# A hybrid decoder step on one core: semaphore clears and one memset moved into the programs of running stages, first weights and first norm started earlier

## The chip, the cores and the metric

The kernel runs on one core of a Trainium2 chip. Its time is the device time of one execution in microseconds (us); the median of several runs is compared. An engine's program is a list of instructions that it takes in order; engines wait for each other by semaphores. PE is TensorE, DVE VectorE, ACT ScalarE, POOL GpSimd, and SP SyncE, which here only issues transfers (DMAs).

## What is computed

One inference step of a one-layer decoder, for a prompt group (1024 tokens) and a sample group (8 sequences of 4 tokens with a paged cache of 4096 keys) that share all weights. All of it is in float32:

```
xn = rmsnorm(x);  [A | B] = groups of xn @ w_in
h  = x + concat(DSA_A(xn), DiffAttn_B(xn)) @ w_out
h2 = h + MemXAttn(rmsnorm(h), mem)
y  = h2 + ConvFFN(rmsnorm(h2))
rmsnorm(x, g) = x * rsqrt(mean(x*x) + 1e-6) * g
```

DSA_A is attention over the 256 keys that an indexer scores highest, DiffAttn_B the difference of two softmax attentions with relative-position bias. Rows of projected keys and values are outputs too.

## The kernel before

The work is a row of stages. Each stage is one block: every engine gets its own program for it, and at the block's end all engines meet (each drains, POOL collects them and releases them) before any starts the next block. The stages up to the feed-forward part are "in" (the input projection), "pb" (prompt differential attention), "sa" (prompt selective attention beside all sample attention), "wo" (output projection, residual, norms of its result and of the memory tokens), "kv" and "mq" (memory projections), then the attention into the memory and its projection.

Semaphores of a stage are made by `Stage.sem`, which appends them to the list `Stage.ended`. Twice, after pb and after sa, `clear_semaphores` (line 177) opens a block of its own in which POOL alone has work, one clear instruction for each semaphore of the list. After wo a third small block holds one DVE memset of QBM, a [128, 1024] tile that the mq stage fills in part (line 3364).

The input projection (`projection_stage` with `first_norm`) goes through steps (chunk of columns j, tile of 128 tokens t), 9 tiles for each chunk; the first chunk is 324 columns wide. A step is 8 pairs of fp32 matmul instructions on PE (the trace counts 16). Interleaved with steps are two helpers:

- `FirstNorm` makes the normalised, transposed input XT tile by tile. ACT squares and sums a tile of x, POOL makes 1/sqrt of the mean, DVE scales the tile (`scale`, line 480) into one of two buffers in KTB, PE transposes it in two halves (line 496) into two PSUM banks, DVE copies each half out and multiplies by the norm's gains (line 468). Tiles 0 to 4 are turned before step 0, tile s + 4 ahead of step s.
- `Setup` loads constants, turns 124 rows of per-column gains into columns (`turn_columns`, `columns`) and makes tables: bias rows for 12 heads, one head per step, on PE (line 332) and DVE (line 363), and page tables for the gathers. It waits for its loads with the semaphore `loaded`.

SP issues in this order: 13 small loads counted by `first` (identity, norm and gain rows), 13 loads counted by `loaded` (two pieces of a constant table, relative bias, gains, lambda, the page table), then the first chunk of w_in in four pieces, piece x when tile x is scaled, because these weights lie where x tiles 0 to 3 lie. ACT issues the nine x tiles, on a queue of its own.

The order of all this is fixed by the Python loops: what stands in a step of a helper comes at that step, on each engine.

Of the kernel before, what the change touches and what calls it, by code (L numbers as in the profile page):

```python
# [22 lines left out]
P = 128  # L23
D = 1024
# [152 lines left out]
def clear_semaphores(nc):  # L177

    with nc.Block() as block:
        @block.gpsimd  # L180
        def _(pool):
            for s in Stage.ended:
                pool.sem_clear(s)
    Stage.ended.clear()

# [27 lines left out]
class Setup:  # L213
# [7 lines left out]
    def __init__(self, nc, ctx, io, M, K):  # L221
# [6 lines left out]
        def place(n):  # L228
# [13 lines left out]
        self.first, self.loaded = S.sem("first"), S.sem("loaded")  # L242
        self.toe_out = [S.sem(f"toe_out{x}") for x in range(4)]
        (self.chain, self.cols_tr, self.rbw_ready, self.bias_mm, self.bias_cp, self.lrow_ready, self.samp_mm,
         self.lam_ready, self.lam_exp) = (S.sem(n) for n in (
             "chain", "cols_tr", "rbw_ready", "bias_mm", "bias_cp", "lrow_ready", "samp_mm", "lam_ready", "lam_exp"))
        self.n_first = self.n_loaded = 0

    def first_loads(self, sp):
# [5 lines left out]

        def rowload(name, src, k):
            load(self.rows[COL[name]:COL[name] + k, :], src.rearrange("(k p) -> k p", p=P))
        load(M.ident[:], io["ident"][:])
        rowload("norm_mix", io["norm_mix"][0], KC)
# [29 lines left out]
    def turn_columns(self, pe):  # L289
        pe.wait_ge(self.first, self.n_first)  # L290
        self.nc.tensor.transpose(self.M.PS[:, 4, 0:NCOL], self.rows[:], self.K("ident")[0:NCOL, 0:NCOL]
                                 ).then_inc(self.cols_tr, 1)

    def columns(self, dve):
# [8 lines left out]
        link(nc.vector.tensor_copy(M.cols[:], M.PS[:, 4, 0:NCOL]))  # L303
# [50 lines left out]
    def dve(self, eng, s, room):  # L354
        nc, M, K = self.nc, self.M, self.K
        link, h = self.link, s - 1
# [3 lines left out]
        if 0 <= h < self.HEADS:  # L360
# [4 lines left out]
        if s == 0:  # L365
# [47 lines left out]
class FirstNorm:  # L413
# [3 lines left out]
    AHEAD = 4  # L417

    def __init__(self, nc, ctx, io, M, K, setup):
# [8 lines left out]
    def sp(self, eng):  # L428
        self.setup.first_loads(eng)
        self.setup.other_loads(eng)  # L430

    def act(self, eng):
        nc, M = self.nc, self.M
        load_x(eng, self.io, M)
        junk = M.PS[:, 0:2, :].rearrange("p b n -> p (b n)")
        for t in range(NT):
# [4 lines left out]
            nc.scalar.activation(junk[0:n, :], M.X[0:n, t, :], ACT.Square,  # L441
# [14 lines left out]
    def dve(self, eng, s):  # L456
# [5 lines left out]
        for t in range(self.copied, min(NT, s + self.AHEAD + 1)):  # L462
# [3 lines left out]
            for b in range(2):  # L466
# [3 lines left out]
                    M.PS[:, 6 + b, 0:4 * n].rearrange("p (c n) -> p c n", c=4),  # L470
# [12 lines left out]
    def pe(self, eng, s):  # L483

        nc, M = self.nc, self.M
        if s == 0:
            self.setup.turn_columns(eng)
        for t in range(self.turned, min(NT, s + self.AHEAD + 1)):
            n = rows_of(t)
            eng.wait_ge(self.scaled, t + 1)  # L490
            for b in range(2):
                if t:
                    eng.wait_ge(self.evac_done, 2 * t - 1 + b)
                for c in range(4):
                    k = 4 * b + c
                    last = nc.tensor.transpose(M.PS[:, 6 + b, c * n:(c + 1) * n],
# [3 lines left out]
        if s == 0:  # L500
            eng.wait_ge(self.sq_done, NT)
# [4 lines left out]
def projection_stage(nc, M, K, name, XT, kc, tiles, w_dram, chunks, w=None, sq=None, beside=None, ahead=None,  # L506
                     following=None, first_norm=None):
# [20 lines left out]
    with ExitStack() as ctx:  # L528
# [20 lines left out]

        def wait_nat(eng, s):  # L550
# [7 lines left out]
        with nc.Block() as block:  # L558
            @block.sync
            def _(sp):  # L560
                def load(j):
# [5 lines left out]
                    if j == 0:  # L567
                        for x, first in enumerate(w_first):
                            if first_norm:
                                sp.wait_ge(first_norm.scaled, x + 1)  # L570
                            sp.dma_start(w[0][:, 2 * x:2 * x + 2, 0:c.width],
# [8 lines left out]
                if first_norm:  # L580
                    first_norm.sp(sp)
                load(0)
# [19 lines left out]
            def _(pe):  # L602
# [15 lines left out]
                for s, (j, t) in enumerate(steps):  # L618
# [9 lines left out]
                    for c in range(kc):  # L628
                        if s == 0 and c == 0 and ahead:
                            pe.wait_ge(*ahead[1:])  # L630
                        elif s == 0 and c % 2 == 0 and not ahead:
                            pe.wait_ge(w_first[c // 2], 16)
                        last = nc.tensor.matmul(M.PS[0:n, s % 3, 0:chunks[j].width],  # L633
                                                XT[:, c, t * P:t * P + n], w[j % 2][:, c, 0:chunks[j].width],
# [881 lines left out]
def selective_and_sample_stage(nc, io, M, K):  # L1516


    with ExitStack() as ctx:
# [1903 lines left out]
```

## Time and profile before

| | us |
|---|---|
| median of 3 runs | 2669.65 (2663.4 to 2672.65) |
| profiled execution, its time | 2665.05 |
| its span | 2663.2 |
| PE busy | 2344.6 (88%) |
| DVE busy | 1105.1 (41%) |
| ACT busy | 767.4 (29%) |
| POOL busy | 725.6 (27%) |

The span is the time from the first to the last instruction of the profiled execution, 1.85 us less than its time. The granted clock of PE was 0.94 of full over the span. A line number with q behind the engine's name (PEq, SPq) is that engine's sequencer: branches, waits and issues of transfers. "Landing" is when a transfer's semaphore has been raised.

### The profile page before, as it was taken

The numbers are of one execution on the slowest core, as the hardware profiler recorded it, in microseconds if no ns is written. First come the engines' busy times: TensorE is split into PE (matmuls) and PEld (weight loads), VectorE is DVE, ScalarE is ACT, GpSimd is POOL, SyncE is SP. The second block draws the span as 40 slices with busy tenths as digits, with TensorE's granted clock in tenths as the row PEclk, the third lists the DMA queues.
The fourth block names the chain that finished last, engine by engine and source line by source line (L and its number), as shares of the span: only waits on it lengthen the run. The fifth ranks groups of instructions, "written<-read, shape, count | busy, mean of one in ns | idle before, by whom it ended". The sixth has DMA issues, their size and how long they took to land. (4 is left out here: it accounts for less than half of the span.)

```text
span 2663.2 us, 32560 instructions
## 1 busy us (share of the span) xinstructions
PE 2344.6 (88%) x12153; PEld 1563.1 (59%) x12173; DVE 1105.1 (41%) x2683; ACT 767.4 (29%) x2065; POOL 725.6 (27%) x767
## 2 busy tenths in 40 slices
PE   7999997767887887877669989898999999999999
PEld 5644444443554555544444434547888888888887
DVE  4489988732445533232321311335334334352001
ACT  3551346643444444433331102411111111110000
POOL 1450222123445454436430001003212212201110
PEclk9999997988889898888789999999999999999999
DMA  3211101035888687755433022220111111122221
GB/s 136 73 60 68 35 7 64 1 111 185 273 270 280 215 276 259 249 159 162 124 111 144 0 79 79 80 81 33 49 40 42 49 33 49 49 63 68 72 62 41
DMA packets 148611, 281.75 MB, mean 106 GB/s; under 512 B 14487, under 2 KB 83783, under 8 KB 148455
## 3 DMA queue, kind: packets, MB, share of 16 engines
q0 software_dynamic: 49408, 176.19, 20.3%
q1 hardware_dynamic: 80758, 90.50, 10.3%
q10 hardware_dynamic: 18288, 12.98, 1.7%
q8 instruction: 99, 1.62, 0.3%
q14 instruction: 58, 0.47, 0.1%
HBM read 261.68 MB, written 17.94 MB: 105 GB/s over the span
## 5 line engine op out<-in xcount | busy, mean ns | idle before, releaser
L633 PE MATMUL PS<-region 128*128 128x512 f32 (+5 forms) x864 | 327.7, 534 | 1.4 <-DMA region<-w_in 1.4
L2730 PE MATMUL PS<-region,ffn_w 128*128 128x264 f32 x1408 | 323.3, 388 | 1.6 <-PEq L2181 1.6
L2730 PEld LDWEIGHTS PS<-region,ffn_w 128*128 128x128 f32 x1408 | 269.3, 191 | 48.6 <-issue 2.0
L1962 ACT COPY region<-PS 128x512 f32<-128x512 f32 x352 | 197.9, 590 | 231.2 <-remote 74.3
L633 PEld LDWEIGHTS PS<-region 128*128 128x128 f32 (+1 forms) x864 | 152.7, 181 | 160.8 <-issue 140.5
L1841 PE MATMUL PS<-ident_f,region 128*128 128x128 f32 x1024 | 173.0, 318 | 81.5 <-ACT region L1962 45.7
L2730 PE MATMUL PS<-region,side 128*128 128x264 f32 x1056 | 243.3, 387 | 1.6 <-POOL side L2687 1.6
L2730 PEld LDWEIGHTS PS<-region,side 128*128 128x128 f32 x1056 | 198.9, 190 | 35.0 <-POOL side L2687 1.7
L1841 PEld LDWEIGHTS PS<-ident_f,region 128*128 128x128 f32 x1024 | 134.6, 163 | 117.0 <-issue 75.4
L930 DVE TENSOR_SCALAR_CACHE_REDUCE mask<-score,cand 128x384 bf16<-128x384 f32 (+2 forms) x198 | 180.9, 942 | 3.4
L1108 POOL DMA_INDIRECT region<-cache_b_k,gather_b x128 | 121.8, 952 | 217.3 <-PE PS L1841 180.2
L2685 POOL TENSOR_TENSOR side<-ffn_w 128x512 f32<-128x512 f32 x22 | 28.8, 1307 | 391.4 <-DMA ffn_w<-w_gate 197.6
L2877 DVE TENSOR_TENSOR ffn_gb<-PS,ffn_u 128x264 f32<-128x264 f32 (+2 forms) x66 | 20.5, 338 | 181.5 <-ACT ffn_u L2841 118.7
L2250 PE MATMUL PS<-side,QTB 128*128 128x512 f32 x192 | 87.1, 604 | 0.9 <-PEq L2606 0.9
L1108 POOL DMA_INDIRECT region<-cache_a_v,gather_a x64 | 61.7, 964 | 95.1 <-PE PS L1924 70.8
L2097 DVE SCALAR_TENSOR_TENSOR sa_oacc<-sa_oacc,sa_alpha,PS 128x512 f32<-128x512 f32 (+1 forms) x48 | 29.5, 614 | 135.4 <-PE PS L1924 101.7
L2320 DVE TENSOR_TENSOR region<-PS,region 128x512 f32<-128x512 f32 (+1 forms) x36 | 24.8, 689 | 137.7 <-PE PS L2250 137.7
L1477 DVE TENSOR_REDUCE sa_a_far_max<-PS 128x1 f32<-128x16 f32 (+6 forms) x56 | 31.9, 569 | 103.2 <-PE PS L1418 81.0
L1108 POOL DMA_INDIRECT region<-cache_b_v,gather_b x64 | 60.3, 941 | 42.8 <-PE PS L1924 20.6
L3066 PE MATMUL PS<-H,ffn_w 128*128 128x264 f32 x308 | 69.8, 386 | 1.3 <-PEq L2674 1.3
L2810 ACT COPY side<-PS 128x264 f32<-128x264 f32 x44 | 16.7, 379 | 181.7 <-PE PS L2730 181.7
L1238 ACT ACTIVATE region<-PS,pb_negmax 128x384 f32<-128x384 f32 (+5 forms) x96 | 54.6, 578 | 49.3 <-DVE pb_negmax L1332 32.3
(444 smaller groups left out, 4023.8 us busy)
## 6 DMA issues: line engine op xcount, KB each, us to landing
ffn_w<-w_gate SPq DMA_DIRECT2D x11, 1024.0 KB, 5.4
ffn_w<-w_up SPq DMA_DIRECT2D x11, 1024.0 KB, 5.5
region<-w_in SPq DMA_DIRECT2D x4, 2048.0 KB, 7.9
ffn_w<-w_down ACTq DMA_DIRECT2D x7, 704.0 KB, 5.6
region<-x_prompt ACTq DMA_DIRECT2D x8, 512.0 KB, 7.1
region<-x_prompt SPq DMA_DIRECT2D x8, 512.0 KB, 11.4
mem_keys<-cache_mem_k SPq DMA_DIRECT2D x8, 512.0 KB, 4.2
mem_values<-cache_mem_v SPq DMA_DIRECT2D x8, 512.0 KB, 7.6
```

Source lines behind the costliest of these rows:

```text
L633: last = nc.tensor.matmul(M.PS[0:n, s % 3, 0:chunks[j].width], XT[:, c, t * P:t * P + n], w[j % 2][:, c, 0:chunks[j].width], start=(c == 0 ...
L930: self.link.send(nc.vector.tensor_scalar(self.mask[:, sc], self.score[:, sc], as_float[:, x:x + 1], 0.0, op, ALU.add, accum_out=self.count ...
L1108: nc.gpsimd.indirect_dma_start(out, None, src, bass.IndirectOffsetOnAxis(ap=table[:, col:col + 1], axis=0)).then_inc(arrived, 16)
L1238: nc.scalar.activation(prob[:, 2 * (n % 2) + k, a:b], slot(piece0[n] + x, b - a)[:, k], ACT.Exp, bias=negmax[:, n % 2, k:k + 1], accum_out ...
L1477: nc.vector.tensor_reduce(far_max[:, e:e + 1], slot(e, 0, lo), axis=AX.X, op=ALU.max).then_inc(far_done, 1)
L1841: last = nc.tensor.transpose(t[:, q * P:(q + 1) * P], keys[:, r * 512 + m * P:r * 512 + (m + 1) * P], K("ident"))
L1962: nc.scalar.copy(dst, M.PS[0:dst.shape[0], T0 + x % 2, 0:dst.shape[1]]).then_inc(t_read, 1)
L2097: nc.vector.scalar_tensor_tensor(oacc[:, 0:kw], oacc[:, 0:kw], alpha[:, x], M.PS[:, L1, 0:kw], ALU.mult, ALU.add).then_inc(o_done, 1)
L2250: last = nc.tensor.matmul(M.PS[:, s % 4, :], lhs(c, t), w[q][:, c, :], start=(c == 0), stop=(c == kc - 1))
L2685: nc.gpsimd.tensor_tensor(ws[:, 0], a21, a22, ALU.add).then_inc(made, 1)
L2730: last = nc.tensor.matmul(M.PS[:, bank, 0:TW], left[:, c, :], right[:, c, :], start=begin and c == 0, stop=(c == KH - 1), skip_group_check ...
L3066: last = nc.tensor.matmul(M.PS[:, bank + x, 0:TW], left[:, c, :], right[:, c, x * TW:(x + 1) * TW], start=begin and c == 0, stop=(c == KH ...
```

## The change

- `clear_semaphores` and both of its blocks are gone. The semaphores that had ended before sa are cleared at the end of POOL's program in sa (58, where there were 56: two semaphores are new); those of sa at the start of POOL's program in wo (38).
- The memset of QBM moves from its own block on DVE to the start of POOL's program in wo.
- The first chunk's weights go to the place of QTA (turned queries, written later in the same stage) and not over x. They need not wait for tiles, and SP issues them third, before the loads of `loaded`.
- The norm_mix rows (8) are turned by themselves, after two loads only; the other 116 columns are turned at step 2, after 11 loads counted by a new semaphore `rest`, which SP issues last.
- Two tiles are turned before step 0 and two more ahead of each step up to step 3, with four PSUM banks for the first three tiles; ACT's squares write their unused result to QTB and not to PSUM.
- The part of `Setup` that DVE did at step 0 is at step 1, together with what was there; bias rows of heads 0 and 1 are both made there.

```diff
@@ Setup
+        load(M.ident[:], io["ident"][:])
+        load(self.rows[0:KC, :], io["norm_mix"][0].rearrange("(k p) -> k p", p=P))
+    def rest_loads(self, sp):
...
+    def turn_columns(self, pe, k):
+        pe.wait_ge(*((self.first, self.n_first) if k == KC else (self.rest, self.n_rest)))
@@ Setup.pe
+        if s == 2:
+            self.turn_columns(eng, NCOL)
@@ Setup.dve
-        if s == 0:
+        if s == 1:
             eng.wait_ge(self.loaded, self.n_loaded)
...
+        if s == 2:
+            self.other_columns(eng)
+        for h in (0, 1) if s == 1 else range(s, min(s + 1, self.HEADS)) if s else ():
@@ FirstNorm
-        junk = M.PS[:, 0:2, :].rearrange("p b n -> p (b n)")
+        self.junk = M.QTB[:].rearrange("p m n -> p (m n)")[:, 0:D]
+    def sp(self, eng, weights):
         self.setup.first_loads(eng)
+        weights()
         self.setup.other_loads(eng)
+        self.setup.rest_loads(eng)
+    def tiles_by(s):
+        return min(NT, 2 * s + 2)
+    def bank(t, b):
+        return b + (4 if t == 1 else 6)
-        if s == 0:
-            eng.wait_ge(self.sq_done, NT)
+        if s == 3:
+            eng.wait_ge(self.setup.cols_read, 2)
@@ projection_stage, sync
-                            if first_norm:
-                                sp.wait_ge(first_norm.scaled, x + 1)
@@ selective_and_sample_stage
+        done = Stage.ended[:before]
+        del Stage.ended[:before]
...
                 pool_part(pool)
+                for s in done:
+                    pool.sem_clear(s)
@@ residual_norm_stage, gpsimd
+                if mem:
+                    nc.gpsimd.memset(M.QBM[:], 0.0)
+                for s in done:
+                    pool.sem_clear(s)
                 for k in range(len(normed)):
@@ build
-                        clear_semaphores(nc)
-            clear_semaphores(nc)
-                            nc.vector.memset(M.QBM[:], 0.0)
+                                             first_w=M.QTA[:].rearrange("p m n -> p (m n)")[:, 0:KC * 324]
```

What stood on POOL at the two places, before. `ISA` are the clears, `DMA` the last gathers of sa, and each branch leads from one block to the next:

```order
L1167 UNCONDITIONAL_BRANCH
L180 UNCONDITIONAL_BRANCH
L183 ISA x56
L179 UNCONDITIONAL_BRANCH
L1540 UNCONDITIONAL_BRANCH
```

And now, from the end of sa to the start of wo:

```order
L1130 DMA region<-cache_a_v,gather_a 128x512 x4
L1569 ISA x58
L1559 UNCONDITIONAL_BRANCH
L2310 UNCONDITIONAL_BRANCH
L2313 MEMSET QBM 128x1024
L2315 ISA x38
L2319 TENSOR_SCALAR wo_ms<-wo_ss 128x1
```

The clears stand behind the last gathers and ahead of wo's first norm; no block is left that holds only them.

SP's program at the start of "in", before:

```order
L253 DMA setup_rows<-ffn_conv_w 66x128
L275 DMA const<-consts 128x754
L275 DMA score<-consts 128x637
L275 DMA score<-rel_bias 32x12 x5
L275 DMA gain_ak<-a_k_norm 128x64
L275 DMA gain_bk<-b_k_norm 128x64
L275 DMA gain_mk<-mem_k_norm 128x128
L275 DMA gain_sub<-diff_subln 128x128
L275 DMA score<-diff_lambda 128x256
L275 DMA score<-page_table 128x256
L571 DMA region<-w_in 128x2x324 [waits n_scaled] x4
```

And now:

```order
L243 DMA ident_f<-ident 128x128
L243 DMA setup_rows<-norm_mix 8x128
L592 DMA QTA<-w_in 128x2x324 x4
L273 DMA const<-consts 128x754
L273 DMA score<-consts 128x637
L273 DMA score<-rel_bias 32x12 x5
```

The weights' four pieces moved from behind the page table to ahead of the constants; the loads of `loaded` keep their order among themselves, and 11 of the small ones that stood ahead of them now follow.

DVE's program around its wait for `loaded`, before (KTB is the scaled tile, region<-PS the copy out of PSUM):

```order
L480 TENSOR_SCALAR KTB<-region,n_rstd 128x1024 [waits n_tr_done,n_rstd_done]
L468 TENSOR_TENSOR region<-PS,cols 128x4x128 [waits n_tr_done] x2
L359 MEMSET work 1x256 [waits setup_loaded]
L367 TENSOR_TENSOR score<-score 128x64 [waits setup_chain] x2
L369 TENSOR_REDUCE score<-score 128x2 [waits setup_chain]
L370 CAST ident_b<-ident_f 128x128
L372 CAST tok_to_row_b<-const 128x128 [waits setup_chain] x2
L480 TENSOR_SCALAR KTB<-region,n_rstd 128x1024 [waits n_tr_done,n_rstd_done,setup_chain]
```

And now, around the same wait and at the turn of the other columns:

```order
L488 TENSOR_TENSOR region<-PS,cols 128x4x128 [waits n_tr_done] x2
L367 MEMSET work 1x256 [waits setup_loaded]
L373 COPY work<-score 32x128 [waits setup_chain]
...
L395 CAST score<-score 128x256
L500 TENSOR_SCALAR KTB<-region,n_rstd 128x1024 [waits n_tr_done,n_rstd_done,setup_chain]
L488 TENSOR_TENSOR region<-PS,cols 128x4x128 [waits n_tr_done] x2
L500 TENSOR_SCALAR KTB<-region,n_rstd 128x1024 [waits n_tr_done,n_rstd_done]
L488 TENSOR_TENSOR region<-PS,cols 128x4x128 [waits n_tr_done] x2
L308 COPY cols<-PS 128x116 [waits setup_cols_tr]
```

Before, five tiles were scaled ahead of the first KTB row behind the wait; now four are copied out before the wait, and the scaling of tile 5 (the first KTB row behind it) stands behind all of `Setup`'s step 1.

## Rows read from the trace of the kernel before

**Rows 1.** Timeline: start us, us, engine, line, operation; in brackets idle before it.

```profile
405.97 0.69 DVE L956 TENSOR_SCALAR mask<-work 128x1024 bf16<-128x1024 f32 x1
407.27 1.01 PE L1186 MATMUL PS<-KTB,QTB 64*128 64x128 f32 x6 [3.19 <-PEq L558]
...
559.00 0.69 ACT L1273 ACTIVATE QTB<-PS,cols 128x512 f32<-128x512 f32 x1 [0.75 <-PE PS L1202]
564.52 0.98 PE L1930 MATMUL PS<-WIs,const 32*128 32x4 f32 x4 [5.56 <-PEq L179]
```

**Rows 2.** Timeline: around the second clear and the memset.

```profile
1375.79 0.95 POOL L1108 DMA_INDIRECT region<-cache_a_v,gather_a  x1 [0.30 <-issue]
1396.51 0.68 DVE L2124 TENSOR_TENSOR mix_s<-PS,mix_s 32x512 f32<-32x512 f32 x1 [2.01 <-PE PS L1954]
1400.45 4.61 PE L2250 MATMUL PS<-side,QTA 128*128 128x512 f32 x5 [3.98 <-PEq L179]
...
1536.74 0.91 DVE L3364 MEMSET QBM<- 128x1024 f32 x1 [0.56 <-PEq L2181]
1537.96 7.48 PE L633 MATMUL PS<-proj_w,memT 128*128 128x512 f32 x12 [3.11 <-PEq L3361]
```

**Rows 3.** Timeline: PE, steps 0, 3 and 4 of "in".

```profile
23.82 4.60 PE L633 MATMUL PS<-region 128*128 128x324 f32 x16 [1.39 <-DMA region<-w_in]
...
41.90 4.53 PE L633 MATMUL PS<-region 128*128 128x324 f32 x16
...
48.13 4.63 PE L633 MATMUL PS<-region 128*128 128x324 f32 x16
```

**Rows 4.** Timeline: SP's issues of two loads.

```profile
5.69 0.43 SPq L275 DMA_DIRECT2D score<-consts  x1
10.85 0.43 SPq L275 DMA_DIRECT2D score<-page_table  x1
```

**Rows 5.** Transfers issued in 0 to 50 us: KB, us from issue to landing.

```profile
score<-consts SPq DMA_DIRECT2D x1, 318.5 KB, 8.9
score<-page_table SPq DMA_DIRECT2D x1, 128.0 KB, 12.0
```

**Rows 6.** Queues, 10 to 14.6 us: packets, MB, time share (q1 is SP's, q10 ACT's).

```profile
q10 hardware_dynamic: 327, 1.21, 66.0%
q1 hardware_dynamic: 326, 0.64, 36.7%
```

**Rows 7.** Queues, 15 to 20 us.

```profile
q1 hardware_dynamic: 865, 0.37, 30.0%
```

**Rows 8.** Timeline: DVE in the first steps.

```profile
11.75 0.29 DVE L303 COPY cols<-PS 128x124 f32<-128x124 f32 x1 [8.77 <-PE PS L291]
12.64 1.42 DVE L480 TENSOR_SCALAR KTB<-region,n_rstd 128x1024 f32<-128x1024 f32 x2
...
22.29 1.28 DVE L468 TENSOR_TENSOR region<-PS,cols 128x512 f32<-128x512 f32 x2
...
25.48 0.75 DVE L480 TENSOR_SCALAR KTB<-region,n_rstd 128x1024 f32<-128x1024 f32 x1
...
30.09 0.20 DVE L363 COPY work<-score 32x128 f32<-32x128 f32 x1
...
33.12 0.75 DVE L480 TENSOR_SCALAR KTB<-region,n_rstd 128x1024 f32<-128x1024 f32 x1
...
36.32 0.20 DVE L363 COPY work<-score 32x128 f32<-32x128 f32 x1
...
37.73 0.74 DVE L480 TENSOR_SCALAR KTB<-region,n_rstd 32x1024 f32<-32x1024 f32 x1
```

**Rows 9.** Stretches: us; busy of PE, PEld, DVE, ACT, POOL; PE clock, DMA share, GB/s.

```profile
398.10:402.40 4.30, 0.00 (x0) 0.00 (x0) 4.20 (x5) 0.95 (x5) 3.03 (x2) 0.97 0.00 0
402.40:403.40 1.00, 0.00 (x0) 0.00 (x0) 0.96 (x2) 1.00 (x6) 0.00 (x0) 0.50 0.00 0
1400.45:1405.60 5.15, 5.15 (x6) 2.15 (x7) 0.57 (x3) 0.00 (x0) 0.00 (x0) 0.50 0.77 264
```

More of the change, by code:

```diff
@@ L174, in store_sem @@
         return Stage.stores.get(f"{self.name}_{n}")
[L177 to L184, printed above, removed]
 COL = {}
@@ L241, in __init__ @@
         self.lam2, self.lam2e, self.lam = place(2), place(2), place(1)
-        self.first, self.loaded = S.sem("first"), S.sem("loaded")
+        self.first, self.loaded, self.rest = S.sem("first"), S.sem("loaded"), S.sem("rest")
         self.toe_out = [S.sem(f"toe_out{x}") for x in range(4)]
         (self.chain, self.cols_tr, self.rbw_ready, self.bias_mm, self.bias_cp, self.lrow_ready, self.samp_mm,
-         self.lam_ready, self.lam_exp) = (S.sem(n) for n in (
-             "chain", "cols_tr", "rbw_ready", "bias_mm", "bias_cp", "lrow_ready", "samp_mm", "lam_ready", "lam_exp"))
-        self.n_first = self.n_loaded = 0
+         self.lam_ready, self.lam_exp, self.cols_read) = (S.sem(n) for n in (
+             "chain", "cols_tr", "rbw_ready", "bias_mm", "bias_cp", "lrow_ready", "samp_mm", "lam_ready", "lam_exp",
+             "cols_read"))
+        self.n_first = self.n_loaded = self.n_rest = 0
     def first_loads(self, sp):
@@ L287, in other_loads @@
         load(self.pt_i, io["page_table"].rearrange("b n -> (b n)").partition_broadcast(P))
-    def turn_columns(self, pe):
-        pe.wait_ge(self.first, self.n_first)
-        self.nc.tensor.transpose(self.M.PS[:, 4, 0:NCOL], self.rows[:], self.K("ident")[0:NCOL, 0:NCOL]
+    def turn_columns(self, pe, k):
+        pe.wait_ge(*((self.first, self.n_first) if k == KC else (self.rest, self.n_rest)))
+        self.nc.tensor.transpose(self.M.PS[:, 3 if k == KC else 5, 0:k], self.rows[0:k, :], self.K("ident")[0:k, 0:k]
                                  ).then_inc(self.cols_tr, 1)
@@ L440, in act @@
                 eng.wait_ge(self.sq_done, t)
-            nc.scalar.activation(junk[0:n, :], M.X[0:n, t, :], ACT.Square,
+            nc.scalar.activation(self.junk[0:n, :], M.X[0:n, t, :], ACT.Square,
                                  accum_out=self.ss[0:n, t:t + 1]).then_inc(self.sq_done, 1)
@@ L461, in dve @@
             self.scale(eng, 0)
-        for t in range(self.copied, min(NT, s + self.AHEAD + 1)):
+        for t in range(self.copied, self.tiles_by(s)):
             n = rows_of(t)
@@ L486, in pe @@
         if s == 0:
-            self.setup.turn_columns(eng)
-        for t in range(self.turned, min(NT, s + self.AHEAD + 1)):
+            self.setup.turn_columns(eng, KC)
+        for t in range(self.turned, self.tiles_by(s)):
             n = rows_of(t)
@@ L548, in projection_stage, with weights @@
         sides = beside(S, evac_done) if beside else []
+        def weights(j):
+            return first_w if j == 0 and first_norm else w[j % 2]
         def wait_nat(eng, s):
@@ L580, in _ @@
                 if first_norm:
-                    first_norm.sp(sp)
-                load(0)
+                    first_norm.sp(sp, lambda: load(0))
+                else:
+                    load(0)
                 for s, (j, t) in enumerate(steps):
@@ L1516, in selective_and_sample_stage @@
 def selective_and_sample_stage(nc, io, M, K):
+    before = len(Stage.ended)
     with ExitStack() as ctx:
@@ L2154, in residual_norm_stage @@
     END = len(steps) + 4
+    before = len(Stage.ended)
     def due(s):
@@ L2171, in residual_norm_stage @@
             "sq_done", "ms_done", "rstd_done", "scaled", "tr_done", "evac_done"))
+        done = Stage.ended[:before] if mem else []
+        del Stage.ended[:len(done)]
         def source(k):
@@ L3360, in build @@
                         to_wo.close()
-                    with nc.Block() as block:
-                        @block.vector
-                        def _(dve):
-                            nc.vector.memset(M.QBM[:], 0.0)
                     def load_mq(eng):
```

40 lines of the change are left out of this document (24 added, 16 removed).

## The prediction, made before the changed kernel was run

> **What bounds the kernel.** I read the page first: PE is busy for 2344.6 of 2663.2 us, and nothing else is above half. So time comes from two sources only, stretches in which PE stands still and the time at which a stage first feeds it. Next I read the timeline at the borders of stages. The reader is to see there how long PE waits from the last instruction of one stage to the first of the next, and to compare an ordinary border with the two that hold a block of clears and the one that holds the memset. Then I read PE's and DVE's timelines up to 50 us, since the rest of the change lies there: step 0 waits for a piece of w_in until 23.82 [rows 3], and DVE first waited until 11.75 for the turned rows of gains [rows 8]. From 28 us PE runs on without a pause through the steps of "in", so what a later step starts earlier or later is kept to the stage's end. Last I read the transfers, because the change puts 1.3 MB ahead of what DVE waits for.
>
> **Part 1: three blocks go.** An ordinary border, from in to pb: DVE ends at 405.97 + 0.69 = 406.66, PE begins at 407.27, that is 0.61 [rows 1]. From pb to sa, ACT ends at 559.69 and PE begins at 564.52: 4.83. The block goes, an ordinary border stays: gain 4.22. From sa to wo DVE ends at 1397.19 and PE begins at 1400.45: 3.26, gain 2.65 [rows 2]. From wo to kv DVE ended 0.56 before 1536.74, at 1536.18, and PE begins at 1537.96: 1.78, gain 1.17. Sum 8.0 us. The 56 clears then cost about 4.2 / 56 = 0.075 us each.
>
> What takes the moved work: 58 clears, 4.4 us, stand behind POOL's last gather, which ends at 1376.7, and the stage lasts until 1397.2; 16 us of cover are left. Behind them nothing of sa is queued on POOL. In wo, POOL now has the memset (0.91 on DVE; on POOL not shown by any row, between 0.9 and 4 us, I take 2) and 38 clears, 2.8, before the first norm. The first norm needs a tile with both halves added, the fifth of the steps, and five steps of eight matmuls at 4.61 / 5 [rows 2] are over 20 us. Both are priced at nothing; without cover they would cost 4.4 and some 5 us. No transfer is moved past them: the gathers of sa start with the stage, 4.2 us earlier like all else.
>
> **Part 2: the start.** What goes: DVE's wait for 13 loads until 11.75, the five tiles that stood ahead of step 0, and the place of w_in's pieces behind the page table. Five tiles took DVE from 12.64 to 22.29, 1.9 each [rows 8]; with two of them ahead, and the gains' rows there early, step 0 can begin at about 12.5, not 23.8 (an estimate from that pace). If that were all, "in" would gain 11 us less the three tiles that now stand between steps, about 7. It isn't all, since DVE's program has one wait moved relative to the tiles. Scaling of tile 5, which PE needs before step 2, stands behind all of Setup's step 1, and that waits for `loaded`. I call L the time at which `loaded` is complete; before, it was 10.85 + 12.0 = 22.9 [rows 4, 5] and DVE came to it at 23.6, so it cost nothing.
>
> From L on, by rows 8: the first part of Setup 1.9 (22.29 + 1.28 to 25.48), the second 3.0 (30.09 to 33.12), one more bias row 0.2, scaling tile 5 0.75, copying out tile 4 1.3, and 0.5 for PE's last half tile: step 2 begins at L + 7.7. Then 4.5 for its matmuls [rows 3], 0.9 until the other columns are turned, 0.9 for DVE to copy and scale them (11.75 to 12.64), 1.4 for a bias row and the page table (36.32 to 37.73), 0.75 and 1.3 for tiles 7 and 6, 0.5: step 3 at L + 17.9. Step 3 to step 4 stays 48.13 - 41.90 = 6.2. So step 4 begins at L + 24.1, where it began at 48.1. The start gains 24.0 - L. DVE can't reach the wait before it has copied out four tiles: w_in's last piece lands near 17 (below), step 0 ends at 18, two tiles at 1.9 make 22. So the gain is never more than 2.
>
> **L now.** In 10 to 14.6 us the two queues moved 326 and 327 packets, one for one, together 1.85 MB or 0.40 MB per us [rows 6]; x and the loads of SP share what the transfer engines give. The weights, 4 x 324 KB, are inserted ahead of the constants and take 3.3 us of it. (Their 0.7 MB follow the weights and take 1.7, so the weights land near 16 to 17.) The constants landed at 5.69 + 8.9 = 14.6 [rows 4, 5]; now 14.6 + 3.3 = 17.9 at the earliest, 19.6 if they come last with x. Behind them the small loads took 22.9 - 14.6 = 8.3; 865 of their packets went in the 5 us from 15 to 20 with hardly anything beside them [rows 7], so 5.4 is their least. L lies between 17.9 + 5.4 = 23.3 and 19.6 + 8.3 = 27.9. I take 25, nearer to the low end, as x is done earlier relative to the small loads than before: the start loses 1.0, and gains 0.7 or loses 3.9 at the ends.
>
> A rule weighed here: the Trainium skill, DMA: Bandwidth & Descriptors, section "Issuing engines are not separate DMA queues", says that copies started by different engines run on the same 16 transfer engines and interleave. The equal packet counts agree with it, 326 to 327. By the rule the start loses 1.0 as above; if SP's queue had bandwidth of its own, L would be under 22 and the start would gain 2.0.
>
> **The clock.** After PE had stood still from 398.1 to 402.4, the granted clock was 0.50, 1.2 GHz of 2.4; after PE had begun dense matmuls at 1400.45 it stayed at 0.50 for 5.15 us, in which half the work was done, so one such fall costs 2.6 [rows 9]. In the start PE would now end step 1 at about 26 (22 and a step), have one bias row and one tile, 2 us, and stand until L + 6.5, about 31.5: a pause of 3.5 us. I take one fall, at 2.0 (the half-speed stretch may begin in work that waits anyhow); the bounds are 0 and 4.4, step 2 at half speed throughout. The Trainium skill, TensorE: Matmul & The Clock Gate, Part 1, says that the throttled state is the default and activity lifts it. That is against this change: a PE that starts early and then has too little to do isn't kept fast. Without any fall the sum below would be better by 2.0.
>
> **Sum.** -8.0 for the borders, +1.0 for L, +2.0 for the clock: -5.0 us. Against the profiled execution, 2665.05, this is 2660. That execution was 4.6 below the median of the three runs, 2669.65, so against the median it is 2664.6, and I forecast 2664. A measurement of this kernel tells a change from none at about 0.3%, 8.0 us: the forecast is no change that can be told, on the faster side.
>
> **Rivals.**
> 1. The small loads don't come late: L at 23.3 and no pause long enough for the clock. For it: page-table and gain loads ran at 0.30 of the engines' time [rows 7], so they have room; against it: the inserted 1.3 MB. The start gains 0.7 to 2.0, sum -8.7 to -10.0, time 2660.
> 2. The other side: SP's queue starves, and PE with it. If x takes most of the time until it has landed and weights, constants and small loads follow one after another, L is 19.6 + 3.3 + 8.3 = 31.2, the pause is near 10 us, and PE does steps 2 and 3 at half speed: -8.0 + 7.2 + 2 x 4.4 = +8.0, or 2677.7, and more with any further delay. For it: loads waited 8.9 to 12.0 us for landing [rows 5]. Against it: the one-for-one packets. The kernel is slower than before once the start loses over 8.0; with the clock down for two steps that is from L = 23.2 on, with the clock up from L = 32.
> 3. The clock moves elsewhere. It was at half when pb began at 402.40 [rows 9], and the start of wo was run at half. All later stages shift by some us against the clock's own changes; one fall of 2.6 more or less at a border, or two at in to pb, where PE works in short groups, makes -7.6 to -10.2 or 0.2 of the sum: 2660 or 2670.
> 4. A clear or the memset isn't covered: it would hold POOL's first norm in wo, or the end of sa; at most 4.4, sum -0.6. The 16 and 20 us of cover speak against it, and I give it no chance of its own.
>
> **How the numbers follow.** Forecast 0.46, with its own range 2660 to 2669; rival 1 0.26; rival 2 0.08; rival 3 0.20, half on each side. The low end is the 10 us of rival 1 with one clock fall less, and some of the 6 us by which single runs lay under the median: 2655. The high end is the forecast with L = 27.9 and 4.4 for the clock, -8.0 + 3.9 + 4.4 = +0.3, or 2670, with 3 for the spread of runs: 2673. Faster by over 0.3%: most of rival 1, half of rival 3, and a little of the forecast's spread, 0.33. Slower by over 0.3%: nearly all of rival 2, 0.07. Within 0.3%: 0.60.
>
> **What would show it.** In the trace after, PE's first instruction of sa comes 0.6 us behind ACT's last one of pb, that of wo 0.6 behind DVE's, that of kv 0.6 behind DVE's copy out of PSUM. Step 0 begins at 12 to 14 us and is held by pieces of w_in. DVE's memset of `work` begins with a wait and stands at L, near 25; step 2 of "in" begins near L + 7.7, step 3 near L + 17.9 and step 4 near 49 to 51. The clock column or the matmuls' pace shows half speed in step 2. The forecast is wrong if DVE doesn't wait for `loaded` (then it is too high by 3), if step 4 begins after 55, or if PE's first instruction at a border still comes 3 us late.

## The result, and the profile after

Six executions of the changed kernel took 2653.26 us in the median (2649.87 to 2658.62), six of the kernel before 2666.56. The ratio is 0.9944 with a 95% interval of 0.9932 to 0.9957: 14.9 us faster (11.5 to 18), more than the 0.3% that can be told apart; the two medians differ by 13.3 us. The forecast was 5 us and no change that can be told. Two executions behind the ratios of this document, at 2908.59 and 9111.32 us, stand far outside the rest and are left out throughout.

The profiled execution has a span of 2653.8 us, 9.4 less than before. Its page differs little; PE is as busy as it was (2343.6 us, before 2344.6).

The borders between stages, which answer to [rows 1, 2] (timeline of the changed kernel: start, us, engine, line, operation, idle before it):

```profile
560.21 0.69 ACT L1295 ACTIVATE QTB<-PS,cols 128x512 f32<-128x512 f32 x1 [0.75 <-PE PS L1224]
...
561.20 0.98 PE L1957 MATMUL PS<-WIs,const 32*128 32x4 f32 x4 [1.03 <-PEq L1189]
...
1394.52 0.68 DVE L2151 TENSOR_TENSOR mix_s<-PS,mix_s 32x512 f32<-32x512 f32 x1 [2.00 <-PE PS L1981]
...
1395.47 0.95 POOL L2313 MEMSET QBM<- 128x1024 f32 x1 [20.70 <-POOLq L1559]
...
1395.52 2.04 PE L2280 MATMUL PS<-side,QTA 128*128 128x512 f32 x2 [1.04 <-PEq L1559]
...
1435.22 0.19 POOL L2319 TENSOR_SCALAR wo_ms<-wo_ss 128x1 f32<-128x1 f32 x1 [38.80 <-ACT wo_junk L2300]
...
1529.70 1.29 DVE L2341 TENSOR_TENSOR region<-PS,cols 128x512 f32<-128x512 f32 x2 [1.18 <-PE PS L2262]
...
1531.31 1.19 PE L655 MATMUL PS<-proj_w,memT 128*128 128x512 f32 x1 [1.65 <-PEq L2211]
```

From the last instruction of the stage to PE's first it is now 0.30, 0.32 and 0.32 us; it was 4.83, 3.26 and 1.78. The gain is 4.53 + 2.94 + 1.46 = 8.9 us. The memset took 0.95 us on POOL, whose first norm in wo came 39.8 us after the stage began.

The start answers to [rows 3, 8]. First PE (timeline of the changed kernel), then what stands behind PE's waits, on DVE, ACT and SP (line 516 transposes a tile, 655 multiplies, 340 makes a bias row):

```profile
18.63 1.36 PE L655 MATMUL PS<-QTA,region 128*128 128x324 f32 x4 [1.29 <-DMA QTA<-w_in]
...
30.19 1.16 PE L516 MATMUL PS<-ident_f,KTB 128*128 128x128 f32 x8 [1.51 <-DVE region L488]
...
31.19 4.53 PE L655 MATMUL PS<-QTA,region 128*128 128x324 f32 x16
...
40.21 1.16 PE L516 MATMUL PS<-ident_f,KTB 128*128 128x128 f32 x8 [2.19 <-DVE region L488]
...
41.21 4.53 PE L655 MATMUL PS<-QTA,region 128*128 128x324 f32 x16
...
48.42 1.52 PE L340 MATMUL PS<-score,work 33*128 33x384 f32 x2 [2.36 <-ACT work L357]
...
50.85 6.84 PE L655 MATMUL PS<-QTA,region 128*128 128x324 f32 x16
```

```profile
23.71 0.27 DVE L367 MEMSET work<- 1x256 f32 x1
...
28.70 0.75 DVE L500 TENSOR_SCALAR KTB<-region,n_rstd 128x1024 f32<-128x1024 f32 x1
...
36.19 0.28 DVE L308 COPY cols<-PS 128x116 f32<-128x116 f32 x1 [3.69 <-PE PS L290]
...
38.71 0.75 DVE L500 TENSOR_SCALAR KTB<-region,n_rstd 128x1024 f32<-128x1024 f32 x1
...
46.78 0.60 ACT L718 COPY in_nat<-PS 128x256 f32<-128x256 f32 x3 [18.60 <-DMA p_idx_k<-in_nat]
...
39.49 0.40 SPq L598 DMA_DIRECT2D region<-w_in  x1
39.93 7.87 SPq L616 DMA_DIRECT2D p_idx_k<-in_nat  x3
```

DVE's memset of `work`, the place of the wait for `loaded`, stands at 23.71 without a pause: the loads were no longer missing. From there to step 2 it is 7.5 us and to step 3 17.5 (forecast from L: 7.7 and 17.9). What was not foreseen comes behind: PE waits 2.36 us for ACT ahead of step 4, and step 4 takes 6.84 us, not 4.63: from 50 to 54 us PE had a granted clock of 0.50. ACT's copies of step 2 waited for step 0's store of `p_idx_k`. SP issues that store behind the second chunk's weights, and these wait until tile 7 is scaled, at 38.71 where it was 33.12 [rows 8]. Step 4 begins at 50.85, before at 48.13, and step 5 at 58.79, before at 53.86.

The second chunk gives back 3.5 us: from its first step to its sixth PE took 110.14 - 79.84 = 30.3 us before and takes 111.56 - 84.77 = 26.8 now. Before, PE waited for a bias row in four of its steps. These are the first and the last of the four in the kernel before (timeline); in the changed one none of these rows has a wait:

```profile
84.73 0.59 PE L332 MATMUL PS<-score,work 33*128 33x384 f32 x1 [0.85 <-DVE work L363]
...
103.61 0.59 PE L332 MATMUL PS<-score,work 33*128 33x384 f32 x1 [0.80 <-DVE work L363]
```

In the diff the loop over heads in `Setup.dve` now makes head s at step s, which PE uses at step s + 1.

### The profile page after: what moved, and what is told of

It is laid out like the page before. It is cut to its first block and busy times, and to the rows that moved or that the text cites. A ratio compares the mean times of both kernels' runs of the same rounds, so it can differ in the third digit from the quotient of the medians.

```text
span 2653.8 us, 32532 instructions
## 1 busy us (share of the span) xinstructions
PE 2343.6 (88%) x12154; PEld 1563.2 (59%) x12174; DVE 1101.2 (41%) x2683; ACT 767.5 (29%) x2065; POOL 725.9 (27%) x768
## 5 line engine op out<-in xcount | busy, mean ns | idle before, releaser
L655 PE MATMUL PS<-region 128*128 128x512 f32 (+3 forms) x720 | 286.5, 552 | 0.0
L1868 PE MATMUL PS<-ident_f,region 128*128 128x128 f32 x1024 | 173.9, 319 | 83.9 <-ACT region L1989 51.5
L655 PEld LDWEIGHTS PS<-region 128*128 128x128 f32 (+1 forms) x720 | 127.3, 181 | 145.3 <-issue 134.3
L1861 PE MATMUL PS<-ident_f,region 128*128 128x128 f32 x256 | 41.6, 300 | 33.3 <-ACT region L1989 22.8
L1130 POOL DMA_INDIRECT region<-cache_a_k,gather_a x64 | 61.8, 965 | 27.8 <-issue 15.7
```

The lines of the kernel that those rows point to most:

```text
L1130: nc.gpsimd.indirect_dma_start(out, None, src, bass.IndirectOffsetOnAxis(ap=table[:, col:col + 1], axis=0)).then_inc(arrived, 16)
L1861: last = nc.tensor.transpose(t[:, q * P:(q + 1) * P], keys[:, q * P:(q + 1) * P], K("ident"))
L1868: last = nc.tensor.transpose(t[:, q * P:(q + 1) * P], keys[:, r * 512 + m * P:r * 512 + (m + 1) * P], K("ident"))
```

## The experiments

All were built on the kernel before or the changed one; the diffs shown are shortened. Each ratio is to the kernel before on the same chip. Chips differ: its median was 2667.68, 2643.42, 2670.01 and 2671.54 us in four sets of runs on three chips. On the chip with the lowest, the changed kernel's stage sa took 807.6 us (e5_after_again), beside 834.3 in its first profile. So only ratios are compared. Single executions spread by 4.4 us about their kernel's mean.

**The parts alone.** The borders' edits on the kernel before, then the start's edits with the three blocks kept:

```diff
-clear_semaphores(nc)            # both, and the block of the memset
+nc.gpsimd.memset(M.QBM[:], 0.0)   # start of wo
+for s in done: pool.sem_clear(s)   # end of sa, start of wo; start of the kernel unchanged
```

> The kernel before with the borders alone changed: clears at the end of sa's and at the start of wo's GpSimd programs, memset in wo's; the start as before. By my sum (4.22 + 2.65 + 1.17) 8.0 us faster than before, ratio 0.9970; by the borders as they stand in the trace after (4.53, 2.95 and 1.65 from PE's last instruction to its first) 9.1 us, 0.9966. If the missing gain lies in the borders, by something that the profile does not show, 13 us or more, 0.995.

Measured: 0.9966 (0.9949 to 0.9982). 

> The borders alone, as in e1_borders: 8.9 us by the gaps of the profile (4.53, 2.94 and 1.46), ratio 0.9966 as before within 0.0015.

Measured: 0.9959 (0.9945 to 0.9973). The gaps in both traces are again 0.30 to 0.32. In e2_start and e13_start_2, with two clears more, the first gap is 4.98 and 4.97 where it was 4.83.

```diff
+first_w, tiles_by, turn_columns(pe, k)   # the changed start
 clear_semaphores(nc)                     # kept, and the memset's block
```

> The kernel before with the start alone changed; the two blocks of clears and the block of the memset stay. By my prediction 3.0 us slower. By the trace after, step 5 of 'in' 4.9 us later and the next chunk 3.5 us less late, since each bias row is made one step ahead: 1.4 us slower, ratio 1.0005, with the second chunk's second step and those behind it free of the 0.85 us wait. If the missing gain lies here, outside of what one profile shows, 4 us or more faster.

Measured: 0.9993 (0.9978 to 1.0009). 

> The start alone, as in e2_start: the second chunk begins 0.3 to 4.9 us later than in the kernel before by how much of steps 2 to 4 falls to half clock, and 3.5 us of bias rows come back: between 3.8 faster and 1.4 slower, ratio 0.9986 to 1.0005, near 0.9993.

Measured: 1.0006 (0.9995 to 1.0017), a little above the expected range. The start alone is worth nothing that can be told. Its PE timeline in e2_start shows where it goes:

```profile
31.25 5.71 PE L665 MATMUL PS<-QTA,region 128*128 128x324 f32 x16
...
41.45 1.94 PE L526 MATMUL PS<-ident_f,KTB 128*128 128x128 f32 x8 [2.19 <-DVE region L498]
...
43.18 6.57 PE L665 MATMUL PS<-QTA,region 128*128 128x324 f32 x16
```

The pauses are those of the changed kernel, but here steps 2 and 3 ran partly at half clock, and step 4 at full.

**The whole again**, unchanged, three times.

> The changed kernel once more, for a second profile and to stand beside the next two. By the first measurement a ratio of 0.9944. The clock in the first 60 us: in its first profile PE stood at half from 48.9 to 55.6; in e2_start and e3_load_later, whose programs are the same up to 20 us, at 30 to 33 and 40 to 47. If the falls are fixed by the program, the second profile shows 48.9 to 55.6 again; if they are partly chance, another place. Without a fall of its own step 5 would begin near 56.

Measured: 0.9939 (0.9916 to 0.9962). 

> The changed kernel a third time, on one chip with the two that follow. If the parts add up, its gain over before is the sum of theirs within 3 us, by profiles 8.9 + 1.4 = 10.3 plus what the clock gives, 10 to 15 in all, ratio 0.9945 to 0.996. If the whole gives more than its parts, 0.994 and the parts sum to 11 or less.

Measured: 0.9954 (0.9938 to 0.9970). 

> The changed kernel a fourth time, beside the two: 0.994 to 0.9955, after 0.9944, 0.9939 and 0.9954.

Measured: 0.9929 (0.9913 to 0.9944), below the expected range. In e5_after_again no half-clock stretch came in the first 60 us, and the store landed sooner, so that PE waited 0.44 us where it had waited 2.36:

```profile
46.39 0.88 PE L340 MATMUL PS<-score,work 33*128 33x384 f32 x2 [0.44 <-ACT work L357]
...
47.81 4.63 PE L655 MATMUL PS<-QTA,region 128*128 128x324 f32 x16
...
53.53 2.72 PE L655 MATMUL PS<-QTA,region 128*128 128x324 f32 x9
```

Step 5 is at 53.53, 5.3 us ahead of the first profile of the same program. So the size of that loss is chance: the program is the same.

A least-squares fit of the 200 executions, with a mean for each set of runs on one chip, gives (one standard error): whole -14.9 +- 1.1 us, borders -10.8 +- 1.1, start -0.1 +- 1.1. The whole exceeds the parts' sum by 4.1 +- 1.9, twice its error: it may be chance, and no run settles it.

**The load and the store.**

```diff
-if t == tiles[0] and j + 1 < len(chunks):
+if t == (3 if first_norm and j == 0 else tiles[0]) and j + 1 < len(chunks):
     load(j + 1)
```

> The changed kernel, but SP issues the second chunk's weights at step 3 and not ahead of the stores of step 0. Theory: step 2's copies on ACT waited for step 0's store, which stood on SP behind that load until 39.9 and landed at 46.7; now the store goes out near 21 and has landed before 30. Step 2's copies come near 36.2, the 2.36 us pause of PE before the bias row goes, step 4 of 'in' begins near 47.3 and not 50.85, at full clock (4.6 and not 6.84 us), and step 5 near 53.3 and not 58.8: 5.0 us faster than the changed kernel. Rival: DVE is what holds step 4 (the tile's copy at 50.6), then step 4 stays at 50 and the time is the changed kernel's.

Measured: 0.9945 (0.9927 to 0.9963), no gain over the changed kernel. The timelines of ACT and PE show that the wait did go, and what took its place:

```profile
36.97 0.60 ACT L718 COPY in_nat<-PS 128x256 f32<-128x256 f32 x3 [9.53 <-PE PS L637]
```

```profile
30.87 5.69 PE L655 MATMUL PS<-QTA,region 128*128 128x324 f32 x16
...
42.78 6.55 PE L655 MATMUL PS<-QTA,region 128*128 128x324 f32 x16
...
51.04 4.63 PE L655 MATMUL PS<-QTA,region 128*128 128x324 f32 x16
```

Steps 2 and 3 ran partly at half clock, and step 4 is back at 51.04. The rows of steps 2 and 3, transposes included, are 4.3 us longer than their like at full clock (an estimate from these rows and those of the changed kernel), which is more than the 3.7 us by which the expectation of 47.3 was missed.

**DVE's tables later.** With the load moved as above:

```diff
 if s == 2:
+    self.tables(link)       # lambda, casts, sample rows, page numbers: were at s == 1
     self.other_columns(eng)
-if 2 <= s < 5:              # gather tables
+if 3 <= s < 6:
```

> The changed kernel with the load of e3_load_later, and with DVE's tables (lambda, casts, sample rows, page numbers: 3.9 us) at step 2 instead of 1 and the gather tables at steps 3 to 5 instead of 2 to 4. Theory: PE's pauses before steps 2 and 3 (1.51 and 2.19 us) are DVE's tables standing ahead of the scaling of tiles 5 and 7. Step 2 begins near 29.7 (31.19), step 3 near 38.5 (41.21), step 4 near 44.8 (50.85), step 5 near 50.6 (58.79), with no half clock between: 2.7 us faster than e3_load_later, 7 to 8 faster than the changed kernel. Rival: the pauses move with the work, since DVE's sum over steps 2 and 3 is what counts; then step 3 stays near 40.5 and little is gained over e3_load_later.

Measured: 0.9935 (0.9912 to 0.9958), steps 2 to 5 at 29.57, 39.00, 45.24 and 50.96 as expected. 

> The kernel of e4_tables_later once more, beside the changed kernel on one chip. Its first profile was 7.8 us ahead of the changed kernel's at the end of 'in', its median 5.4 us below. Expected: ratio to before 0.993, 4 to 8 us below e5_after_again. If the gain at the start is given back by the clock, it equals e5_after_again within 2 us.

Measured: 0.9936 (0.9912 to 0.9959). Beside e5_after_again that is 0.8 us in the medians, where 4 to 8 had been expected; here a half-clock stretch (38 to 42 us) put step 5 at 53.09, and e5_after_again had none. 

> The kernel of e4_tables_later a third time: 1.2 us later at the end of 'in' than e15_columns_again with a full clock, 2.9 with a half-clock stretch before step 3; ratio 0.992 to 0.994.

Measured: 0.9913 (0.9897 to 0.9929), better than expected; PE's first instruction of pb comes at 402.88, 2.9 us behind that of e15_columns_again, as expected with a half-clock stretch. By the fit over all three runs of it, this version is 18.2 +- 1.2 us faster than the kernel before; with the load alone moved it is 14.4 +- 1.6. With the tables moved and the load in its old place:

> DVE's tables later as in e4_tables_later, but the second chunk's load ahead of step 0's store as in the changed kernel. Theory: tile 7 is scaled near 36.4, the load goes out there, the store lands some 7 us behind it, near 43.7; ACT's copies of step 2 and the bias row's copy follow by 45.0, PE's bias row waits until 45.3 where e4_tables_later ran it at 43.8, so step 4 begins near 46.8 instead of 45.24 and step 5 near 52.5: 1.5 us behind e4_tables_later if the clock stays up. If the load's place costs nothing, step 4 is at 45.2 again.

Measured: 0.9941 (0.9924 to 0.9958). ACT's copies of step 2 do wait for the store, until 43.14, but step 3 also ran partly at half clock (5.21 us) and hid that; step 4 is at 47.08. What the load's place costs at a full clock stays unshown (by the fit this version is 15.1 +- 1.6 us faster than the kernel before).

**The other columns later as well.**

```diff
-if s == 2:
+if s == 3:                  # DVE: behind the tiles of step 3
     self.other_columns(eng)
+if s == 3 and first_norm:   # PE: behind step 3's matmuls
+    pe.wait_ge(first_norm.setup.cols_read, 2)
-if s == 3:                  # PE: this wait stood ahead of the tiles of step 3
-    eng.wait_ge(self.setup.cols_read, 2)
```

> The kernel of e4_tables_later with the copy of the other columns on DVE behind the tiles of step 3 instead of ahead of them, and PE's wait for them behind step 3's matmuls. Theory: PE's last pause over 1 us there (1.61 before tile 7) shrinks to 0.4, step 3 begins near 37.8 (39.0 there), step 4 near 44.0, step 5 near 49.8, and no half-clock stretch comes between 25 and 60. Its time is 2 to 6 us below e11_whole. Rival: the stretch comes although no pause over 1 us is left, then pauses are not what decides it.

Measured: 0.9910 (0.9893 to 0.9927), 11.6 us below e11_whole in the medians, where 2 to 6 had been expected. PE's timeline, and the stretch from 20 to 60 us (busy of PE, PEld, DVE, ACT, POOL; PE clock, DMA share, GB/s):

```profile
28.73 1.16 PE L519 MATMUL PS<-ident_f,KTB 128*128 128x128 f32 x8 [0.44 <-DVE region L491]
...
37.00 1.16 PE L519 MATMUL PS<-ident_f,KTB 128*128 128x128 f32 x8 [0.44 <-DVE region L491]
...
38.00 4.53 PE L656 MATMUL PS<-QTA,region 128*128 128x324 f32 x16
...
44.23 4.63 PE L656 MATMUL PS<-QTA,region 128*128 128x324 f32 x16
...
49.95 4.63 PE L656 MATMUL PS<-QTA,region 128*128 128x324 f32 x16
```

```profile
20.00:60.00 40.00, 38.69 (x174) 25.87 (x173) 24.88 (x84) 10.22 (x44) 1.79 (x4) 1.00 0.21 62
```

> The kernel of e14_columns_later once more. If the start's order is worth what the traces show, 7 to 9 us at the end of 'in', it lies 6 to 12 us below e17_whole_again, ratio 0.991 to 0.9925; if the first measurement was luck in later stages, 0.9935 or above.

Measured: 0.9904 (0.9888 to 0.9920), 2647.32 us beside 2652.73 for the changed kernel (e17_whole_again). By the fit this version is 22.6 +- 1.5 us faster than the kernel before and 7.7 +- 1.7 faster than the change. The traces agree: PE's first instruction of pb comes at 399.8 and 400.0 us, beside 406.0 in the mean of the eight profiles with the changed start, load and rows, and 407.8 in the mean of the three with the old start.

Over all traces of the early part: with PE's pauses of 1.5 and 2.2 us (the changed start) half clock came between 28 and 56 us in 8 of 9; with 0.4 and 1.6 (tables later) in 3 of 4; with nothing over 0.5 (columns later) in 0 of 2; with the old start in 0 of 3. In e10_rows_late (below), whose pauses there are 1.37, 1.18 and 0.72, it came too. So the pauses and the half clock go together in these 19 profiles; the groups are small, and no pause was shown to bring a fall each time.

**Prices of blocks, clears and memsets**, on the changed kernel:

```diff
+for _ in range(8):                       # between pb and sa: empty blocks
+    with nc.Block() as block: ...
+    for _ in range(3): for s in Stage.ended: pool.sem_clear(s)   # block between sa and wo
-    nc.gpsimd.memset(M.QBM[:], 0.0)
+    9 times, each waiting for the one before   # start of wo
```

> The changed kernel with eight blocks without work between pb and sa, one block that clears sa's semaphores three times over between sa and wo (114 clears and those of the added semaphores' list), and nine memsets of QBM on GpSimd at the start of wo where one stood. Theory: a block alone costs about 0.3 us (the memset's block cost 1.17 with 0.91 of work), so PE's first instruction of sa comes 1.68 + 2.4 = 4.1 us behind its last of pb, and the clears 0.07 us each, so that of wo comes 2.95 + 0.3 + 8.0 = 11.2 behind. If an empty block costs a whole border of 0.6, 6.6 us at the first. The memsets take 8 us more of GpSimd and nothing of PE: the first norm of wo is at the same distance, 39.7 us, from the stage's start.

```profile
557.14 0.69 ACT L1295 ACTIVATE QTB<-PS,cols 128x512 f32<-128x512 f32 x1 [0.75 <-PE PS L1224]
...
560.79 0.98 PE L1957 MATMUL PS<-WIs,const 32*128 32x4 f32 x4 [3.69 <-PEq L3372]
...
1372.97 0.68 DVE L2151 TENSOR_TENSOR mix_s<-PS,mix_s 32x512 f32<-32x512 f32 x1 [2.01 <-PE PS L1981]
...
1382.58 1.19 PE L2281 MATMUL PS<-side,QTA 128*128 128x512 f32 x1 [9.65 <-PEq L3379]
...
1382.54 9.02 POOL L2314 MEMSET QBM<- 128x1024 f32 x9 [29.74 <-POOLq L3379]
...
1421.99 0.19 POOL L2321 TENSOR_SCALAR wo_ms<-wo_ss 128x1 f32<-128x1 f32 x1 [30.43 <-ACT wo_junk L2301]
```

Eight blocks: 560.79 - 557.83 = 2.96, less 0.30, is 0.33 us each. The block of clears: 1382.58 - 1373.65 = 8.93, less 0.32 and 0.33, is 8.28 for 114 clears, 0.073 each. The nine memsets hold nobody: the first norm comes 39.5 us into the stage. From PE's own last instruction the distances are 3.69 and 9.65, where 4.1 and 11.2 had been expected. (The expectation's 1.68 counts from the start of PE's last group; from its end the border of the changed kernel is 1.03. Its 2.95 is the gain at the second border, which is itself 1.04.)

```diff
+for s in 6 * done: pool.sem_clear(s)      # end of sa: 348 clears, not 58
+45 memsets at the start of wo, one empty block between pb and sa
```

> The changed kernel with one empty block between pb and sa, the 58 clears at the end of sa's GpSimd program made six times over, and 45 memsets of QBM at the start of wo. Theory: the clears, some 32 us behind 1369, outlast the stage's other engines (1394.5) by 7 us or so, and wo begins that much later; the memsets end near 45 us into wo, 6 us behind the place at which the first norm was wanted (39.7), and the first norm on GpSimd comes that much later; PE loses less, having tiles to multiply. The empty block costs 0.3 us (0.6 by the rival).

```profile
1364.95 0.68 DVE L2151 TENSOR_TENSOR mix_s<-PS,mix_s 32x512 f32<-32x512 f32 x1 [2.01 <-PE PS L1981]
...
1371.32 45.37 POOL L2314 MEMSET QBM<- 128x1024 f32 x45 [23.97 <-POOLq L1559]
...
1371.36 2.04 PE L2281 MATMUL PS<-side,QTA 128*128 128x512 f32 x2 [6.44 <-PEq L1559]
...
1419.80 0.19 POOL L2321 TENSOR_SCALAR wo_ms<-wo_ss 128x1 f32<-128x1 f32 x1 [3.11 <-issue]
```

348 clears (24.0 us, 0.069 each) outlast sa by 5.4 us, and wo begins that late; 45 memsets delay the first norm to 48.4 us into wo, some 9 late. Both covers are real and have an end: 18 us in sa, and 39 in wo before POOL's norm is late. PE did not feel that: its waits for scaled tiles in wo come to 3.5 us in this run and in the changed kernel. The empty block cost 0.33 again (1.36 us from PE's end, where it was 1.03). e8_prices, e9_cover and e10_rows_late were executed once each, and are read for such distances only.

**Bias rows.** On the changed kernel:

```diff
-for h in (0, 1) if s == 1 else range(s, min(s + 1, self.HEADS)) if s else ():
+for h in range(s - 1, min(s, self.HEADS)) if s else ():
```

> The changed kernel with each bias row's copy on DVE at the step at which PE uses it, as before the change, and not a step ahead. Theory: PE waits 0.80 to 0.86 us for it in four steps of the second chunk (steps 9 to 12), as in the kernel before, so the way from the second chunk's first step to its sixth is 30.3 us, and 26.8 in the changed kernel. Rival: the wait went for another reason and stays away.

```profile
83.43 3.72 PE L655 MATMUL PS<-region 128*128 128x256 f32 x16
...
88.33 0.59 PE L340 MATMUL PS<-score,work 33*128 33x384 f32 x1 [0.85 <-DVE work L373]
...
107.21 0.59 PE L340 MATMUL PS<-score,work 33*128 33x384 f32 x1 [0.80 <-DVE work L373]
...
113.75 3.72 PE L655 MATMUL PS<-region 128*128 128x256 f32 x16
```

The four waits are back, and the way is 113.75 - 83.43 = 30.3 us, as before the change; in the changed kernel it is 26.8. The rival is out.

## Why the prediction was wrong

The forecast was -5.0 us and the runs gave -14.9. By the profiles the borders gave 0.9 us more than the sum had, the start 4.2 more (-1.2 where it said +3.0), and the later stages 3.6 +- 3.0 that had no term. The step that failed is the sentence that PE runs on without a pause from 28 us, so that a later or earlier step is kept to the stage's end: four waits of PE stood there, and the change took them away. Another 3.1 us of the 10.7 between forecast and measured median is the base: the kernel before had a median of 2669.65 us in three executions, and 2666.56 in six. "Faster by over 0.3%", which came true, had been given 0.33.

**Borders: mechanism right, the gain 0.9 us too small.** The ordinary border was taken from in to pb, 0.61; at the three places it is 0.30 to 0.32. So -8.9, not -8.0. The clears and the memset cost nothing, as said (memset 0.95 us, forecast 2).

**`loaded`: right mechanism, L too late.** The page table was issued at 14.5 and took 8.2 to land, so L was 22.7, below the low end of 23.3. The constants did wait longer (15.6 us to landing, before 8.9 [rows 5]) and landed at 20.1, later than both bounds of the forecast. But SP's small loads overlapped with them: the page table, issued 3.7 us later than before, took 3.8 less to land, 2.7 us behind the constants and not the 5.4 that had been called the least. So L did not move. DVE came to the wait at 23.7, late itself, since w_in's last piece held step 0 until 18.6. At step 3 the start had gained 0.7 where the sum said a loss of 1.0. The first sign of being wrong, that DVE doesn't wait for `loaded`, was there. (In the kernel before six tiles were scaled ahead of this wait, not five: tile 5 at 21.63. Tile 5's scaling did go behind the wait, as the sum has it.)

**"Step 3 to step 4 stays 6.2": wrong.** It took 9.6 in the first profile and 6.7 in e5_after_again, which has no half clock there. I followed DVE and PE and left out that the second chunk's load on SP waits for the scaling of tile 7, with step 0's store queued behind it and ACT behind the store. The order on SP stood in the code; the rows of ACT were not read.

**"From 28 us PE runs on without a pause": wrong, and the largest miss.** PE waited four times, 3.3 us in all, for bias rows between 84 and 104 us, a stretch of which I had read no row ([rows 8] end at 38). The diff's loop over heads removed that; I counted the row as moved work, not as a wait that goes. e10_rows_late shows it: 3.5 us, which the sum had at nothing.

**Clock in the start: about right in size.** Step 5 stood on average at 56.1 us over the eight profiles with the changed start, load and rows (53.53 to 58.79), 2.6 behind the one without half clock; I had taken 2.0. Some 0.5 of the 2.6 is not the clock but a longer wait of ACT for the store (PE's wait behind it was 0.44 to 2.36 us). But one fall was no fixed cost: a stretch fell in step 2, 3 or 4, three of the eight profiles had two, and one had none.

So the start comes to 56.13 - 53.86 - 3.51 = -1.2 by the profiles and to -0.1 +- 1.1 by the runs; the forecast said +3.0.

**The clock in later stages (rival 3): seen in mq, in favour of the change; in sum not clear of noise.** Summed over the stages from pb on, from PE's first instruction of one to that of the next, three profiles with the blocks (before, e2_start, e13_start_2) took 12.5 us more than the ten without them on like chips, with a standard error of 3.0: stage sa alone ranges from 830.6 to 841.5 us among the ten. The gaps are 8.9 of it. Of the other 3.6, 1.1 lies in mq and 1.4 in the feed-forward stage, where no instruction was changed. The same first 6 us of mq in the kernel before, and then in the changed kernel (stretches; the clock is third from the end):

```profile
1571.81:1577.81 6.00, 6.00 (x10) 2.57 (x11) 0.00 (x0) 0.00 (x0) 0.00 (x0) 0.72 0.01 3
```

```profile
1565.76:1571.76 6.00, 6.00 (x14) 2.74 (x15) 0.00 (x0) 0.00 (x0) 0.00 (x0) 1.00 0.01 3
```

mq took 71.55 us with that stretch and 69.85 without; it came in 2 of 3 profiles with the blocks and in none of the 14 without, on any chip, nor in e8_prices and e9_cover, which have blocks before sa and wo but none before kv. The feed-forward stage is less clear: without blocks it took 849.7 to 849.8 us in twelve profiles, but 851.4 and 851.5 in two on the third chip, as long as with them (850.2, 850.8 and 852.3). The sum -8.9 - 1.2 - 3.6 = -13.7 is within the errors of -14.9, but its last term could as well be nothing or 7. Why a stretch of half clock comes 35 us behind a longer border is not settled, and so the cause of that part of the gain stays open. The profiled pair alone, -9.4, was one draw: the changed kernel's profile was 2.7 us above its median.

Rival 1 came nearest on L (23.3), but it had no half clock in the start and no wait that goes, and its 2660 us is too high as well; rival 2 did not occur. The range missed because it had nothing for the four waits, and allowed the clock to cost, and hardly to give back, at places where PE stands still less.

## What to carry to other kernels

An edit that makes something one step earlier may remove a wait far from the place at which it was meant: list the consumer's waits in the whole stage before saying that it runs on without one. Follow each delayed event to every engine that waits for it, SP's queue and the stores behind a load included. On PE, count pauses amid dense work as a risk to its clock too: a start that is earlier but broken up was worth nothing that could be told, and without its pauses, with the load moved behind the store, it was worth 7.7 +- 1.7 us.

## What the runs showed of the hardware

- The profiles of one and the same program differ in where half-clock stretches come: the changed kernel's step 5 began between 53.53 and 58.79 us. In the 188 executions whose clock is known, with means for each kernel and set taken out, the time was 1.64 +- 0.10 us lower for each 0.001 more of mean granted clock.
- From 10 to 14.6 us the two queues again moved packets one for one (queues of the changed kernel: packets, MB, time share):

```profile
q10 hardware_dynamic: 384, 1.38, 75.3%
q1 hardware_dynamic: 387, 0.47, 28.3%
```

  That agrees with the rule of the Trainium skill weighed above (DMA: Bandwidth & Descriptors, "Issuing engines are not separate DMA queues"); as SP's packets were the smaller ones, it moved a third of the bytes.
- An empty block costs 0.33 us, a semaphore clear on GpSimd 0.07, a 128x1024 memset there 0.95 to 1.0.
- The same store behind the same load landed so that ACT went on at 46.78 in one profile and at 44.74 in another.
- In e1_borders, whose program up to there is that of the kernel before, a half-clock stretch came between 92 and 96 us, right behind a pause of 0.80 us in which PE waited for a bias row: a step of 16 matmuls took 5.41 us where its like takes 3.72. In the kernel before and in e12_borders_2, with the same pause, that step ran at full clock.
